# Adaptive modulation at the start of a two-block kernel: TensorE pieces with 512 moving columns, and one more vector piece and subtraction on VectorE

## What is computed

```python
c_act = jax.nn.silu(c)                                  # c: (1, 1024)
mod = c_act @ w_ada[layer] + b_ada[layer]               # w_ada: (1024, 3072)
shift, scale, gate = jnp.split(mod, 3, axis=-1)
h = rms_norm(x, norm_in_gain[layer]) * (1.0 + scale[:, None, :]) + shift[:, None, :]   # x: (512, 1024)
proj = h @ w_in[layer]                                  # the first 512 columns are the first half of q
q, k, v, z_attn, xbc, dt_raw, z_ssm = jnp.split(proj, splits, axis=-1)
```

## Time and profile before

| | us |
|---|---|
| median of three executions | 1977.61 |
| lowest, highest | 1975.96, 1978.41 |
| the profiled execution | 1975.55 |
| its span, first to last instruction | 1973.8 |
| PE busy in the span | 1898.0 (96%) |
| VectorE, ScalarE, GpSimd busy | 881.0, 755.1, 622.3 |

### The profile page before, as it was taken

The page is one execution under the profiler, slowest core; times in us unless marked ns, Lnnn a source line. Parts: engine busy times, 40 slices in busy tenths (PEclk is TensorE's granted clock), DMA queues, the critical chain, the costliest instruction groups (busy, mean ns, idle before and its releaser), DMA issues.

```text
span 1973.8 us, 23386 instructions
## 1 busy us (share of the span) xinstructions
PE 1898.0 (96%) x9337; PEld 1554.2 (79%) x9337; DVE 881.0 (45%) x1324; ACT 755.1 (38%) x1274; POOL 622.3 (32%) x204
## 2 busy tenths in 40 slices
PE   8999999999899899999999999999989999999998
PEld 7787888868777666787888888888778887888886
DVE  4511354542875435866253333336356344222334
ACT  3324445446323434335343222226545343222232
POOL 2343112222112422430343434343310143444432
PEclk7999999999999999999999999999899999999999
DMA  7523111111112221230223232332210022223221
GB/s 281 179 86 109 51 44 43 44 43 64 43 63 98 69 77 57 72 117 1 75 88 105 85 105 86 106 102 73 81 42 1 33 86 96 96 89 102 87 104 75
DMA packets 81079, 160.97 MB, mean 82 GB/s; under 512 B 5721, under 2 KB 7902, under 8 KB 80990
## 3 DMA queue, kind: packets, MB, share of 16 engines
q1 hardware_dynamic: 80990, 159.75, 24.5%
HBM read 157.64 MB, written 2.10 MB: 81 GB/s over the span
## 4 chain that ended last, share of the span: by engine, by line
PE 89%; DVE 6%; ACT 3%; issue 1%; POOL 1%; DMA 0%; SPq 0%; DVEq 0%; ACTq 0%
PE PDT L573 13%; PE PDT L575 13%; PE PDT L574 13%; PE PDT L584 8%; PE PDT L586 8%; PE PDT L585 8%; PE PM L1128 3%; PE PM L906 2%; PE PM L886 2%; PE PM L1079 2%; PE PM L920 2%; PE PM L1098 1%; PE PDT L1098 1%; PE PM L816 1%; PE PM L619 1%
## 5 line engine op out<-in xcount | busy, mean ns | idle before, releaser
L1704 POOL TENSOR_TENSOR wlo<-wraw,whi 128x2048 fp32r<-128x2048 f32 (+4 forms) x155 | 610.4, 3945 | 1315.2 <-ACT whi L1231 1281.4
L1231 ACT ACTIVATE whi<-wraw 128x2048 fp32r<-128x2048 f32 (+2 forms) x133 | 247.7, 1863 | 544.2 <-PE PDT L575 331.6
L584 PE MATMUL PDT<-hhi,whi 128*128 128x512 f32 x736 | 290.2, 394 | 5.0 <-ACT mh_r L1350 5.0
L586 PE MATMUL PDT<-hhi,wlo 128*128 128x512 f32 x736 | 287.7, 391 | 0.0
L585 PE MATMUL PDT<-hlo,whi 128*128 128x512 f32 x736 | 287.4, 391 | 0.0
L573 PE MATMUL PDT<-whi,hhi 128*128 128x512 f32 (+1 forms) x676 | 270.9, 401 | 6.0 <-DVE hlo L1811 5.3
L575 PE MATMUL PDT<-whi,hlo 128*128 128x512 f32 (+1 forms) x676 | 262.6, 388 | 0.0
L574 PE MATMUL PDT<-wlo,hhi 128*128 128x512 f32 (+1 forms) x676 | 262.4, 388 | 0.0
L573 PE MATMUL PDT<-whi,mh_hi 128*128 128x512 f32 x512 | 202.5, 396 | 0.0
L575 PE MATMUL PDT<-whi,mh_lo 128*128 128x512 f32 x512 | 202.5, 396 | 0.0
L574 PE MATMUL PDT<-wlo,mh_hi 128*128 128x512 f32 x512 | 202.4, 395 | 0.0
(11 more groups left out here) (329 smaller groups left out, 2573.4 us busy)
## 6 DMA issues: line engine op xcount, KB each, us to landing
wraw<-in_mlp_w SPq DMA_DIRECT2D x64, 1024.0 KB, 5.1
wraw<-in_w_in SPq DMA_DIRECT2D x26, 1024.0 KB, 5.1
wraw<-in_even_w_in SPq DMA_DIRECT2D x16, 1024.0 KB, 5.3
w_ada<-in_w_ada SPq DMA_DIRECT2D x12, 1024.0 KB, 13.4
wraw<-in_w_out SPq DMA_DIRECT2D x8, 1024.0 KB, 5.1
wraw<-in_even_w_out SPq DMA_DIRECT2D x4, 1024.0 KB, 5.0
wraw<-in_odd_w_o SPq DMA_DIRECT2D x4, 1024.0 KB, 5.2
wraw<-in_odd_w_uq SPq DMA_DIRECT2D x3, 768.0 KB, 4.4
```

Of the source, the lines that this page charges most:

```text
L584: mm(bank, sth, hi[:, k0 + k, :], start=start and k == 0, stop=False)
L586: last = mm(bank, stl, hi[:, k0 + k, :], start=False, stop=stop and k == 3)
L1231: nc.scalar.activation(whi[base % 2][:, 0:n], wraw[base % 2][:, 0:n], ACT.Copy).then_inc(S("w_hi"), 1)
L1704: part = g.tensor_tensor(wlo[base % 2][:, cols], wraw[base % 2][:, cols], fl(whi[base % 2][:, cols]), ALU.subtract)
```

## The change

On PE, `weigh` now holds `silu_c` as the stationary operand, spread over 128 columns (`silu_w`, a new tile that DVE fills by one copy), and moves the piece, four matmuls of 512 columns. The result is a row, the same in all partitions, in a bank of PSUM of its own for each chunk. `total` becomes one matmul with ones stationary and `acc` moving. The row must then be turned: DVE copies one partition of it to `mod_rows`, and PE's new `columns(half)` turns it by eight matmuls with one moving column. Piece 4 goes from PE to DVE. The first `wlo` goes from POOL to DVE, and POOL's next subtraction waits for that one. On SP the loads keep their order except that piece 3 now comes ahead of the first `w_in` unit and piece 7 ahead of the second; the waits for pieces 8 to 11 follow the new owners of the buffers.

```diff
--- before.py
+++ after.py
@@ -192,6 +192,8 @@
     silu_c = arena("silu_c", [P, KT], 66.5)
     colc = arena("colc", [P, 32], 66.625)
     modc = arena("modc", [P, 2, KT], 66.75)
+    silu_w = arena("silu_w", [P, KT, P], 93)
+    mod_rows = arena("mod_rows", [1, 4, 512], 24)
     gate = arena("gate", [P, DM], 98)
     row_c = arena("row_c", [P, DM], 52)
 
@@ -451,13 +453,12 @@
 
         for t in range(TT):
             load(xres[:, t, :], x[0, t * P:(t + 1) * P, :], f"x_loaded{t}")
-        for n in range(3):
+        for n in range(4):
             ada(n)
         first_unit(0)
-        for n in range(3, 7):
+        for n in range(4, 8):
             ada(n)
         first_unit(1)
-        ada(7)
         with nc.allow_non_contiguous_dma(reason="512 positions"):
             load(pos_i[:, :], positions_2[0].rearrange("(t p) -> p t", p=P))
         load(prm_a[C_CW:C_CW + 48, :], conv_w[0].rearrange("j (k p) -> (j k) p", p=P))
@@ -472,13 +473,13 @@
         load(small[:, 32:48], d_skip[0].partition_broadcast(P))
         for h in range(2):
             unit(2 + h, h, 4, 512, w_in_v[:, 4 * h:4 * h + 4, 512:1024])
+        sp.wait_ge(S("dve_pieces"), 3)
+        ada(8)
+        sp.wait_ge(S("dve_pieces"), 4)
+        ada(9)
         sp.wait_ge(S("pe_pieces"), 3)
-        ada(8)
-        sp.wait_ge(S("dve_pieces"), 3)
-        ada(9)
-        sp.wait_ge(S("pe_pieces"), 4)
         ada(10)
-        sp.wait_ge(S("dve_pieces"), 4)
+        sp.wait_ge(S("dve_pieces"), 5)
         ada(11)
         load(row_b[:, :], b_ada[0][2 * DM:3 * DM].partition_broadcast(P), "row_gate")
         columns("k", w_in_v, 2, DM)
@@ -807,32 +808,37 @@
                                                ident[:, :])
                 last.then_inc(S("xt_turned"), 1)
 
-        def weigh(n, bank, col, fresh):
+        def weigh(n, bank):
 
             pe.wait_ge(S(f"ada_loaded{n}"), 16)
             w = wview(ADA_SLOTS[n], 4, 512)
-            for j in range(4):
-                for k in range(4):
-                    last = mm(PM[:, bank, col + j:col + j + 1], w[:, k, j * P:j * P + P], silu_c[:, k:k + 1],
-                              start=fresh and j == 0 and k == 0, stop=False, skip_group_check=True)
+            for k in range(4):
+                last = mm(PM[:, bank, :], silu_w[:, 4 * (n % 2) + k, :], w[:, k, :], start=k == 0, stop=False)
             last.then_inc(S("pe_pieces"), 1)
 
-        def total(chunk, bank, col, fresh, made):
+        def total(chunk, bank, fresh, made):
 
             pe.wait_ge(S("dve_pieces"), made)
-            for j in range(4):
-                last = mm(PM[:, bank, col + j:col + j + 1], acc[chunk][:, j * P:j * P + P], ones[:, 0:1],
-                          start=fresh and j == 0, stop=True, skip_group_check=True)
-            return last
+            mm(PM[:, bank, :], ones[:, :], acc[chunk][:, :], start=fresh, stop=True).then_inc(S("mod_sum"), 1)
+
+        def columns(half):
+
+            for s in range(2):
+                pe.wait_ge(S("mod_row"), 2 * half + s + 1)
+                for j in range(4):
+                    last = mm(PM[:, 2 * half, 4 * s + j:4 * s + j + 1],
+                              mod_rows[0:1, 2 * half + s, j * P:j * P + P], ones[0:1, 0:1],
+                              start=s == 0 and j == 0, stop=True, skip_group_check=True)
+            last.then_inc(S("mod_sum"), 1)
 
         for t in range(TT):
             turn_x(t)
-        pe.wait_ge(S("c_ready"), 1)
-        weigh(0, 0, 0, True)
-        weigh(2, 0, 4, False)
-        total(0, 0, 0, False, 1)
-        total(1, 0, 4, False, 2).then_inc(S("mod_sum"), 1)
-        weigh(4, 1, 0, True)
+        pe.wait_ge(S("c_ready"), 2)
+        weigh(0, 0)
+        weigh(2, 1)
+        total(0, 0, False, 1)
+        total(1, 1, False, 2)
+        columns(0)
 
         def first_half(h):
 
@@ -849,9 +855,14 @@
                     mm(PD[f], st, hhi[:, 4 * h + k, :], start=h == 0 and k == 0, stop=False)
                     mm(PD[f], st, hlo[:, 4 * h + k, :], start=False, stop=False)
                 if h == 0 and f == 1:
-                    weigh(6, 1, 4, False)
+                    weigh(6, 3)
+            if h == 0:
+                total(2, 2, True, 4)
+                total(3, 3, False, 5)
             unit_wait(h)
             for f in range(4):
+                if h == 0 and f == 1:
+                    columns(1)
                 for k in range(4):
                     last = mm(PD[f], wl[:, k, f * P:f * P + P], hhi[:, 4 * h + k, :], start=False,
                               stop=h == 1 and k == 3)
@@ -861,8 +872,6 @@
                 last.then_inc(S("w_used"), 1)
 
         first_half(0)
-        total(2, 1, 0, False, 3)
-        total(3, 1, 4, False, 4).then_inc(S("mod_sum"), 1)
         first_half(1)
         two_units("q", 2, 1, 0, 2, True)
         pe.wait_ge(S("params"), 16 * N_PARAMS)
@@ -870,7 +879,7 @@
         nc.tensor.transpose(PM[:, 2, P:P + ROWS_B], prm_b[0:ROWS_B, :], ident[0:ROWS_B, 0:ROWS_B]).then_inc(S("tr_done"), 1)
         chunks("k", 2, True)
         for i in range(2):
-            pe.wait_ge(S("dve_pieces"), 6 + 2 * i)
+            pe.wait_ge(S("dve_pieces"), 7 + 2 * i)
             mm(PM[:, i, :], ones[:, :], acc[4 + i][:, :], start=True, stop=True).then_inc(S("gate_sum"), 1)
         chunks("v", 2, False)
 
@@ -1743,9 +1752,7 @@
             g.memset(freq[:, j:j + 1], THETA ** (-2.0 * j / 16))
         for j in range(16):
             g.memset(freq[:, 8 + j:9 + j], THETA ** (-2.0 * j / 32)).then_inc(S("freqs"), 1)
-        pool.wait_ge(S("dve_pieces"), 2)
-        lo(0, 0, 0)
-        pool.wait_ge(S("dve_pieces"), 4)
+        pool.wait_ge(S("w_split"), 1)
         pairs("q", 2)
         pairs("k", 2)
         pairs("v", 2)
@@ -1845,6 +1852,7 @@
 
         dve.wait_ge(S("c_ready"), 1)
         link(v.tensor_copy(colc[:, :], PM[:, 3, 8:40]))
+        v.tensor_copy(silu_w[:, :, :], silu_c[:, :].unsqueeze(2).to_broadcast([P, KT, P])).then_inc(S("c_ready"), 1)
 
         def turned_x(t):
             dve.wait_ge(S("xt_turned"), 2 * t + 2)
@@ -1868,9 +1876,13 @@
         def modulation(half):
 
             cols = slice(4 * half, 4 * half + 4)
-            dve.wait_ge(S("mod_sum"), half + 1)
-            v.tensor_tensor(modc[:, 1, cols], PM[:, half, 4:8], colc[:, B_SHIFT + 4 * half:B_SHIFT + 4 * half + 4], ALU.add)
-            link(v.tensor_tensor(modc[:, 0, cols], PM[:, half, 0:4], colc[:, B_SCALE + 4 * half:B_SCALE + 4 * half + 4],
+            for s in range(2):
+                dve.wait_ge(S("mod_sum"), 3 * half + s + 1)
+                v.tensor_copy(mod_rows[0:1, 2 * half + s, :], PM[0:1, 2 * half + s, :]).then_inc(S("mod_row"), 1)
+            dve.wait_ge(S("mod_sum"), 3 * half + 3)
+            bank = PM[:, 2 * half, :]
+            v.tensor_tensor(modc[:, 1, cols], bank[:, 4:8], colc[:, B_SHIFT + 4 * half:B_SHIFT + 4 * half + 4], ALU.add)
+            link(v.tensor_tensor(modc[:, 0, cols], bank[:, 0:4], colc[:, B_SCALE + 4 * half:B_SCALE + 4 * half + 4],
                                  ALU.add))
             v.scalar_tensor_tensor(out=modc[:, 0, cols], in0=modc[:, 0, cols], scalar=1.0,
                                    in1=colc[:, B_GAIN + 4 * half:B_GAIN + 4 * half + 4], op0=ALU.add, op1=ALU.mult)\
@@ -1893,12 +1905,16 @@
         weigh(1, True)
         weigh(3, True)
         modulation(0)
-        weigh(5, True)
+        weigh(4, True)
+        dve.wait_ge(S("dve_pieces"), 3)
+        weigh(5, False)
         weigh(7, True)
+        dve.wait_ge(S("w_hi"), 1)
+        v.tensor_tensor(wlo[0][:, :], wraw[0][:, :], fl(whi[0][:, :]), ALU.subtract).then_inc(S("w_split"), 1)
         modulation(1)
         for n in range(8, 12):
             if n % 2:
-                dve.wait_ge(S("dve_pieces"), n - 4)
+                dve.wait_ge(S("dve_pieces"), n - 3)
             weigh(n, n % 2 == 0)
         dve.wait_ge(S("tr_done"), 2)
         v.tensor_copy(col_a[:, 0:ROWS_A], PM[:, 2, 0:ROWS_A]).then_inc(S("tr_read"), 1)
```

## The result

| | before | after |
|---|---|---|
| median of 6 executions | 1977.64 us (1975.96 to 1978.41) | 1965.97 us (1964.17 to 1970.58) |
| profiled execution | 1975.55 us, span 1973.8 | 1970.58 us, span 1968.9 |
| first matmul of the first unit | 37.86 | 29.24 |
| first matmul of unit 2 ("the mark") | 73.70 | 63.34 |

The ratio is 0.9945 with a 95% interval of 0.9932 to 0.9958: 11.7 us less by the medians, 10.9 us by the ratio, and inside the range forecast (1964 to 1973, likeliest 1967.8).

What follows compares the result with a forecast made beforehand. TensorE, busy 96% in fixed order, was taken as the bound. The first product 8.9 us earlier and the work after it put unit 2 9.8 us earlier: 1967.8 us against the median, range 1964.0 to 1973.0.

Steps and rivals of the forecast that it cites:

- The chain to the first product: Up to the first unit: earlier piece 3 and new-form pieces bring the first product to 28.95 instead of 37.86 us.
- The form's working: TensorE's pieces: the 512-column form saves nothing at equal clock, but keeps the upper clock, 3.44 us a piece.
- 2.7 are the load, ... 4.4 piece 4: First product 8.9 us earlier: 2.7 load, 1.8 TensorE's being ready and one-matmul totals less the turning, 4.4 piece 4.
- just covered by TensorE, with 1.1 us left: First unit: piece 4 and the subtraction on VectorE end at 43.5, before TensorE's totals end at 44.6 us.
- The second modulation: Before unit 1: scale read at 47.45; GpSimd's subtraction until 48.1 holds a VectorE step some 0.5 us.
- the forecast's slower branch: Behind the second turning: twelve low products take 4.6 us, to 51.9, if the clock falls at about 48, otherwise 2.8.
- Rival B: Before unit 1: GpSimd's unit-2 subtraction makes the last `hlo` 4.6 us late; gain 5.2, 1972.4 us; chance 0.12.
- Rival C: TensorE's pieces: 512-column float32 passes are not dense work for the clock; slower, 1983 us; chance 0.05.
- Rival A: TensorE up to unit 2: the upper clock is held throughout; gain 10.7 to 12.1, about 1966 us; chance 0.14.
- the shift carries through: From unit 2's first matmul on, TensorE waits on nothing edited, so the end shifts equally, 9.8 us.

Runs made afterwards that it cites:

- e_oldform2: The changed kernel with TensorE's pieces and totals put back to the one-column form, second run of that code: 1973.25 us, ratio 0.9977 against the kernel before.
- r_after: The changed kernel run again, same code: 1967.81 us, ratio 0.9943 against the kernel before.
- e_load: The kernel before with only the load order changed, pieces 3 and 7 one place earlier: 1978.11 us, ratio 1.0000.
- e_poollow: The changed kernel with the first low-half subtraction back on GpSimd: 1971.29 us, ratio 0.9965 against the kernel before.
- e_split: The changed kernel with GpSimd's subtractions for units 1 to 4 written out, units 1 and 2 in four parts each: 1968.30 us, ratio 0.9949 against before.
- e_best4: The changed kernel with the totals' diagonal read by VectorE, GpSimd's subtractions in parts and high products ordered k outside: 1966.32 us, ratio 0.9936 against before.
- e_pe4: The changed kernel with piece 4 back on TensorE in the 512-column form: 1970.22 us, ratio 0.9959 against the kernel before.
- e_diag: The changed kernel without row copies and turning; VectorE reads the totals' diagonal from PSUM: 1968.64 us, ratio 0.9958 against the kernel before.

## Why the prediction was right

**The chain to the first product.** Piece 3 was weighed from 21.09 (said: about 21.0), the pieces ran at 0.43 us an instruction (7.03 us against 6.9), the scale was read at 27.02 (26.75), the first product started at 29.24 (28.95). The form's working was no saving at equal clock and all of it through the clock. Both halves show: piece 6 took 3.60 us in the new form and 3.63 in the old, at the upper level each, and pieces 0 and 2 took 10.24 us in `e_oldform2` and 7.03 in `r_after`.

**Its division into terms** was the weak step. "2.7 are the load, ... 4.4 piece 4" reads as if each could be had alone. `e_load` gained nothing, because TensorE was busy with the old form's pieces and totals until piece 4 ended. No run takes the load order out of the changed kernel, so what it is worth there is not shown. Piece 4's 4.4 us are those of the old form at 1.2 GHz (it ran to 37.86, the preparation was done at 33.4); in the new form putting it back costs 2.2 us at the first product and nothing that shows at the mark. The edits take turns covering one another, and only their sum was right.

**The low half on VectorE** was costed at nothing, "just covered by TensorE, with 1.1 us left". Covered it was (43.53, said 43.5; the totals ended at 44.70, said 44.6), though by 0.6 us, since the first low product started at 44.13. But the step missed what it removes: with the read at 27, GpSimd's subtraction would have held `modc` for 3.09 us (`e_poollow`). The working saw this collision at the second modulation and didn't look for it at the first, where the earlier trace rows gave the unit's `whi` and with it the start of GpSimd's part.

**The second modulation.** Read at 47.54 (47.45), GpSimd until 48.39 (48.1), the hold 0.45 us (0.5), the clock falling at about 47.7 (48), low products to 51.9 (51.9): the forecast's slower branch, step by step. Behind it the level was up again by 51.5 and stayed, so the mark came at 63.34, where the working had 63.3 for that case and 64.1 as its middle: 10.4 us earlier instead of 9.8. Which level an execution has behind the turning was not foreseen but left open, rightly: in `r_after` it stayed up.

**Rival B**, an `hlo` caught by GpSimd: it did not come in the changed kernel; the last `hlo` starts at 52.92 and GpSimd's next subtraction at 54.13. Its condition was the right one: here the small step was held too, so both started together. Where `hf` itself was held, in `e_split` and `e_best4`, the last `hlo` was caught (1.64 and 1.65 us). The hold falls on operations with two SBUF inputs (0.61, 2.97, 3.09, 3.25, 3.32 us where 0.16 is usual, and those two `hlo`) and on `hf`, SBUF to SBUF (1.49 instead of 0.55), and not on those that read PSUM. The Trainium skill ("VectorE: DVE Perf Modes", "Two Vector instructions with no wait between them") says that the second of two SBUF inputs, or the one input of an instruction in a 2-port mode, is read through an interface shared with GpSimd. The rows agree as far as they go. With GpSimd's subtraction in one piece, the held step ended 0.01 to 0.03 us behind it each time.

**Rival C**, 512-column float32 passes not counting for the clock, is wrong: the clock is 1.00 at 17 us, and in `e_pe4`, where it fell at 26.5, it came back inside piece 4 (0.58 in the half microsecond from 29.5, 1.00 in the next). **Rival A** needed the clock held in the idle time before the first product; it fell at 27 in this profile.

**From the mark to the end** the prediction said that the shift carries through. By the medians it does: 11.7 us against 10.4 in the one profile. In that profile itself it doesn't. The start of the same instruction, before and after: 186.0 and 175.7, 501.0 and 490.8, 989.1 and 979.7, 1371.8 and 1364.0, 1536.8 and 1530.3, 1920.7 and 1915.7. Some 5 us of the 10 are lost on the way, nearly all behind 490 us, in steps of up to 1.6 us. One of them, the stretch of 1370 to 1450, in the changed kernel and in `e_split`, whose code is the same there:

```profile
1370.00:1450.00 80.00, 71.59 (x344) 58.49 (x342) 27.45 (x45) 41.69 (x94) 25.68 (x6) 0.91 0.26 86
```

```profile
1370.00:1450.00 80.00, 69.94 (x334) 56.43 (x332) 29.97 (x52) 40.91 (x95) 24.43 (x6) 0.94 0.23 76
```

The clock was 0.91 in the one and 0.94 in the other (0.94 in before). `e_split` ended 12.5 us earlier than before, at 1908.2, with the same mark as the changed kernel; `r_after`, the very same code, started that last instruction at 1919.2 in its profile, 1.5 us early with its mark 9.1 us early, though its median held the gain. So its expectation, an end 9 to 12 us early, failed. Both profiled executions of this code are the slowest of their six. In the fourteen profiles the execution time less the mark lies between 1899.8 and 1909.4 us: highest in `r_after`, `e_best4` and the changed kernel, lowest in `e_split`. The medians and `e_split` speak for a loss that belongs to the single execution and not to the change; that is argued, not shown, and what sets it in an execution, I can't say. That the forecast's time came out rests on the medians, and its agreement within 2 us is in part luck, since what follows the mark varies by 9.6.

## What to carry to other kernels

Where small matmuls stand between dense ones, ask first what clock they run at and what they leave behind: the 512-column form was no cheaper per piece at equal clock, and saved 5.1 us on two pieces (3.2 against `e_oldform2`) because it kept the clock. When a GpSimd tensor operation of some microseconds may overlap a chain of small VectorE steps, look at which of them have two SBUF inputs, and put the GpSimd work elsewhere, or read from PSUM. Splitting it only moved the hold here, and let it catch a later step. Don't price parts that cover one another singly: the first, alone, may measure nothing. And before a mark that moved is put down to an edit, look at the granted clock up to it: in `e_diag` and `e_load` the clock moved it by more than the edit did.

## What was not expected of the hardware

The same 64 instructions (32 one-column matmuls) at the same place took from 9.79 to 13.65 us from one execution to the next, by when the upper level was lost (14.5 to 19.6 us from the start). One-column matmuls with one partition of stationary data cost what those with 128 did, 1.94 us for sixteen instructions against 1.84. And the turning sometimes cost the clock and sometimes not: the twelve low products behind it took 4.61 us in the changed kernel and 3.03 us in `r_after`, from the same code:

```profile
47.23 1.94 PE L829 MATMUL PM<-ones,mod_rows 1*128 1x1 f32 x16
49.10 3.03 PE L867 MATMUL PDT<-hhi,wlo 128*128 128x512 f32 x12
```
